# Seven products instead of eight for the second matrices of two MLPs

## The chip, the cores and the metric

One core of a Trainium2 chip runs the whole program, in float32. The metric is the time of one execution on the device, in microseconds (us); smaller is better.

## What is computed

A first block (attention and a layer of 16 experts) is followed by a second block of two layers. Each layer of the second block mixes 256 tokens of width 1024 and then applies an MLP with a hidden width of 4096. The change touches only the two MLPs on the 256 tokens:

```python
def _mlp(h, w1, w2):
    return jnp.square(jax.nn.relu(h @ w1)) @ w2
...
        x = _layer_norm(alpha * x + g2 * _mlp(x * (1 + sc2) + sh2, mlp_w1[i], mlp_w2[i]), ln2_g[i], ln2_b[i])
```

h is 256 x 1024, w1 is 1024 x 4096, w2 is 4096 x 1024.

## The kernel before

TensorE (PE) multiplies, VectorE (DVE), ScalarE (ACT) and GpSimd (POOL) do the rest, SyncE (SP) issues the weight transfers. Every engine has its own program, executed in order; the order is written out by hand, and engines wait for each other on counting semaphores. All weights go through `ring`, 8 slots of 3072 columns; `feed` issues the transfer of piece n as soon as piece n - 8 is released (`released`), and `arrived` is the wait for a piece. PSUM, the target of the matmuls, has 8 banks of 512 columns. `link` makes DVE wait for its own operation, for where the next one reads its result.

The function `mlp` (L2267) is called twice: for the first layer as mlp_x (about 1884 to 2100 us), for the second as mlp_n (about 2287 us to the end). The hidden width is cut into GROUPS = 16 groups of 256 columns, each with a piece of w1 (`ids[1, g]`, 8 x 256 columns of a slot) and a piece of w2 (`ids[2, g]`, 2 x 1024 columns). LATE = 3 groups at the end are treated apart, so that the first half of the tokens is finished while PE still works on the second.

The first matrix is multiplied by Strassen's scheme in Winograd's form: tokens (2 halves), inner width (2 halves) and the group's columns (2 halves) make 2 x 2 blocks, and seven block products stand for eight. Their operands are the blocks of the transposed tokens `H` and four sums of them `T[1]` to `T[4]` (made once, L2376 to L2379), and the blocks `W` of the weights and four sums (made by DVE for each group in `add_weights`, L2386 to L2390). Two sums lie in the slot behind the piece, one over block 21, the fourth in `fourth`. A block product is four matmuls of 128 columns, since the inner half width is 512. `first(g)` on PE issues the seven products, 28 matmuls, into two banks: 0 and 1 for even groups, 2 and 3 for odd ones. `combine(g)` on DVE adds the products into the four blocks of the hidden layer (L2402 to L2406), then relu and square go into `h1` in one operation (L2412).

The second matrix is multiplied directly: `second(g, t, half)` (L2327) multiplies 128 tokens with 512 output columns in two matmuls of 512 columns, one for each 128 of the group's inner width. The four combinations of t and half add up over all groups in banks 4 to 7. PE's order is first(0), then for each g first(g+1) and the four second(g). In the last three groups only t = 0 is done in this loop, and t = 1 follows, one half after the other.

DVE's order is the weight sums of g+1, then combine(g). After group 8 (GROUPS // 2) `ln_gain` multiplies the residual x by the gain of the layer norm before it and adds the shift, two operations of 1024 columns for each of the two token tiles. At the end DVE multiplies each bank by the gate `gB`, adds ALPHA times x (`gated`, L1542 and L1543), takes statistics and normalizes.

Of the kernel before, what the change touches and what calls it, by code (L numbers as in the profile page):

```python
# [120 lines left out]
def build(nc, A):  # L121
    ctx = ExitStack()
    with nc.Block(no_gpsimd_drain=True) as block, ctx:
# [39 lines left out]
        combined = Count(sem("mlp_combined"))  # L163
        square_done = Count(sem("square_done"))
# [2102 lines left out]
        def mlp(name, layer, s, ids, banks_free, input_normed, prefetch=None, beside=None, tail=None, finish=None):  # L2267
# [4 lines left out]
            fourth = sb(f"{name}_fourth", [2, 4, P], st)  # L2272
# [7 lines left out]
            tsb, wsb, fb, cb, qb = (turned_sums.take(1), weight_sums.take(2 * GROUPS), first_done.take(GROUPS),  # L2280
                                    combined.take(GROUPS), square_done.take(GROUPS))
# [5 lines left out]
            def weights(g):  # L2287

                w = slot(ids[1, g], KC * 2 * P).rearrange("p (k f) -> p k f", k=KC)
                rest = ring[:, ids[1, g] % SLOTS, KC * 2 * P:SLOT].rearrange("p (i k f) -> p i k f", i=2, k=4)  # L2290
                W = {"11": w[:, upper, here], "12": w[:, lower, here], "21": w[:, upper, there], "22": w[:, lower, there]}
                sums = {1: rest[:, 0, :, :], 2: rest[:, 1, :, :], 3: W["21"], 4: fourth[:, g % 2, :, :]}
                return W, sums

            @block.tensor
            def _(pe):
# [5 lines left out]
                def first(g):  # L2302
                    arrived(pe, ids[1, g])
                    if g >= 2:
                        pe.wait_ge(combined.sem, cb + g - 1)
                    W, sums = weights(g)
                    bank = 2 * (g % 2)
                    for n, (b, at, lhs, rhs) in enumerate(((0, 0, W["11"], H["11"]), (0, 1, W["12"], H["21"]),
                                                           (1, 2, W["22"], T[4]), (0, 3, sums[3], T[3]),
                                                           (1, 0, sums[1], T[1]), (0, 2, sums[2], T[2]),  # L2310
                                                           (1, 1, sums[4], H["22"]))):
                        if n == 2 and g == 0:
                            pe.wait_ge(turned_sums.sem, tsb + 1)
                        if n == 3:
                            pe.wait_ge(weight_sums.sem, wsb + 2 * g + 1)
                        if n == 6:
                            pe.wait_ge(weight_sums.sem, wsb + 2 * g + 2)
                        for k in range(4):
                            last = nc.tensor.matmul(ps[:, bank + b, at * P:at * P + P], lhs[:, k, :], rhs[:, k, :],  # L2319
                                                    start=(k == 0), stop=(k == 3), skip_group_check=True)  # L2320
                    last.then_inc(first_done.sem, 1)
                    released[ids[1, g]] = (first_done.sem, fb + g + 1)

                def second(g, t, half):
                    w2 = slot(ids[2, g], 2 * D).rearrange("p (k f) -> p k f", k=2)
                    for fc in range(2):
                        last = nc.tensor.matmul(ps[:, 4 + 2 * t + half, :], h1[:, g % 4, fc, t * P:(t + 1) * P],  # L2327
                                                w2[:, fc, 512 * half:512 * half + 512], start=(g == 0 and fc == 0),
# [3 lines left out]
                early = GROUPS - LATE  # L2332
                first(0)
                for g in range(GROUPS):
                    if g + 1 < GROUPS:
                        first(g + 1)
                    arrived(pe, ids[2, g])
                    pe.wait_ge(square_done.sem, qb + g + 1)
                    if g == 0:
                        banks_free(pe)  # L2340
                    for t in range(NT if g < early else 1):
                        for half in range(2):
                            last = second(g, t, half)
                    if g < early:
                        last.then_inc(mlp_used.sem, 1)
                        released[ids[2, g]] = (mlp_used.sem, used + g + 1)
                last.then_inc(mlp_used.sem, 1)
                for half in range(2):
                    for g in range(early, GROUPS):
                        last = second(g, 1, half)  # L2350
                    last.then_inc(mlp_used.sem, 1)
                for g in range(early, GROUPS):
                    released[ids[2, g]] = (mlp_used.sem, used + early + 3)
# [19 lines left out]
            def _(dve):  # L2373
                run_t.ev(dve, "dve")
                run_t.finished(dve)
                nc.vector.tensor_tensor(T[1], H["12"], H["11"], ALU.subtract)  # L2376
                link(dve, nc.vector.tensor_tensor(T[3], H["22"], H["12"], ALU.subtract))
                link(dve, nc.vector.tensor_tensor(T[2], H["22"], T[1], ALU.subtract))
                nc.vector.tensor_tensor(T[4], H["21"], T[2], ALU.subtract).then_inc(turned_sums.sem, 1)  # L2379

                def add_weights(g):
                    arrived(dve, ids[1, g])
                    if g >= 2:
                        dve.wait_ge(first_done.sem, fb + g - 1)
                    W, sums = weights(g)
                    nc.vector.tensor_tensor(sums[1], W["21"], W["22"], ALU.add)  # L2386
                    link(dve, nc.vector.tensor_tensor(sums[3], W["11"], W["21"], ALU.subtract))
                    nc.vector.tensor_tensor(sums[2], sums[1], W["11"], ALU.subtract).then_inc(weight_sums.sem, 1)
                    dve.wait_ge(weight_sums.sem, wsb + 2 * g + 1)
# [336 lines left out]
```

## Time and profile before

| what | us |
|---|---|
| median of 3 runs | 2513.24 (2512.06 to 2516.07) |
| the profiled execution | 2514.77 |
| its span | 2513.0 |
| PE busy in the span | 2188.3 |
| DVE busy in the span | 682.7 |
| PE, L2327, mlp_x and mlp_n | 112.3 and 112.4 |

The span is the time from the first to the last instruction in the profiled execution, and the profile's times count from its start. A float32 matmul stands in the records as two matmuls and two weight loads (PEld), so 128 matmuls of L2327 in one MLP are 256 records. The granted clock is given as a share of full speed: 1.00 is 2.4 GHz, 0.50 is 1.2 GHz, and between them lies a stretch that had both.

### The profile page before, as it was taken

To read this page: it belongs to the slowest core of one execution; us is meant where nothing else is said; L and a number is where in the kernel's file an instruction comes from. 1 tells how busy PE (TensorE), PEld (TensorE's weight loads), DVE (VectorE), ACT (ScalarE), POOL (GpSimd) and SP (SyncE) were. 2 spreads that over 40 slices of the span, in tenths; PEclk is the share of its full clock that TensorE was granted. 3 is DMA by queue.
4 is the path that set the end of the run, shared out by engine and by line. 5 is a ranking of instruction groups with operands and counts; after the bars stand their busy time and mean duration, and the time that the engine had idled before them with its cause. 6 is when DMAs were issued, how large, how long until landed. Compare 5 with 4: busy or idle time off the path is not lost.

```text
span 2513.0 us, 29663 instructions
## 1 busy us (share of the span) xinstructions
PE 2188.3 (87%) x12828; PEld 1189.4 (47%) x12828; DVE 682.7 (27%) x1319; ACT 211.4 (8%) x495; POOL 41.4 (2%) x109
## 2 busy tenths in 40 slices
PE   8988889878768978978978977978999999989998
PEld 6544353333323424433433424435557776646775
DVE  1332212221311021021011032022335434075344
ACT  1221110000100000000000000011110000060000
POOL 0000000000000000000000000000000003000000
PEclk9999999989899989999999999989899999999999
DMA  8879999999999999999999999993218554324450
GB/s 314 335 280 390 420 407 424 424 424 422 424 420 419 415 420 412 416 419 413 414 420 417 413 424 422 398 415 116 97 48 257 172 188 184 138 90 143 158 177 34
DMA packets 154819, 799.52 MB, mean 318 GB/s; under 512 B 15587, under 2 KB 71626, under 8 KB 101634
## 3 DMA queue, kind: packets, MB, share of 16 engines
q1 hardware_dynamic: 144504, 783.43, 77.5%
q10 hardware_dynamic: 10186, 14.16, 1.7%
q8 instruction: 108, 1.77, 0.3%
q14 instruction: 21, 0.17, 0.0%
HBM read 795.40 MB, written 7.19 MB: 319 GB/s over the span
## 4 chain that ended last, share of the span: by engine, by line
PE 70%; DMA 17%; DVE 7%; issue 3%; ACT 2%; SPq 1%; ACTq 0%; DVEq 0%
PE ps L288 12%; PE ps L1868 8%; PE ps L2327 8%; PE ps L2319 8%; DMA ring<-in_mlp_w 7%; PE ps L321 6%; PE ps L1836 5%; PE ps L2038 4%; PE ps L1841 3%; DMA ring<-in_w_up 3%; PE ps L418 2%; PE ps L1889 2%; PE ps L1877 2%; DVE expert_work L1911 2%; PE ps L2030 2%
## 5 line engine op out<-in xcount | busy, mean ns | idle before, releaser
L1836 PE MATMUL ps<-ring,xe 128*32 128x512 f32 x2048 | 297.2, 643 | 84.4 <-DMA ring<-in_w_up 30.2
L1868 PE MATMUL ps<-ring,expert_work 128*32 128x512 f32 x1408 | 236.4, 688 | 11.5 <-ACT expert_work L1898 11.0
L1841 PE MATMUL ps<-ring,xe 128*32 128x256 f32 x2048 | 207.3, 464 | 2.8 <-issue 2.8
L1841 PEld LDWEIGHTS ps<-ring,xe 128*32 128x32 f32 x2048 | 74.8, 111 | 174.0 <-issue 173.1
L1836 PEld LDWEIGHTS ps<-ring,xe 128*32 128x32 f32 x2048 | 61.4, 114 | 191.4 <-issue 94.6
L1868 PEld LDWEIGHTS ps<-ring,expert_work 128*32 128x32 f32 x1408 | 59.0, 121 | 155.0 <-issue 132.0
L2038 PE MATMUL ps<-ring,c_qT 128*128 128x512 f32 x256 | 114.1, 598 | 11.2 <-DMA ring<-in_mlp_w 11.2
L2030 PE MATMUL ps<-hT,ring 128*128 128x256 f32 x512 | 114.8, 382 | 6.6 <-DMA ring<-in_mlp_w 6.6
L2327 PE MATMUL ps<-ring,mlp_n_h 128*128 128x512 f32 x256 | 112.4, 592 | 0.0
L2327 PE MATMUL ps<-ring,mlp_x_h 128*128 128x512 f32 x256 | 112.3, 592 | 0.0
L2030 PEld LDWEIGHTS ps<-hT,ring 128*128 128x128 f32 x512 | 96.0, 190 | 28.5 <-DMA ring<-in_mlp_w 11.0
L1848 PE MATMUL ps<-cst,expert_work 128*128 128x128 f32 x64 | 18.1, 436 | 96.6 <-DVE expert_work L1915 96.6
L2152 DVE TENSOR_TENSOR c_qT<-c_qT 128x512 f32<-128x512 f32 x16 | 11.1, 693 | 323.6 <-ACT c_qT L2102 323.6
L321 PE MATMUL ps<-hT,ring 128*128 128x256 f32 x384 | 84.1, 380 | 3.2 <-DMA ring<-in_na_w_qkv 2.2
L2038 PEld LDWEIGHTS ps<-ring,c_qT 128*128 128x128 f32 x256 | 47.3, 190 | 74.6 <-issue 74.6
L1911 DVE RECIPROCAL expert_work<-expert_work 128x512 f32<-128x512 f32 (+1 forms) x32 | 81.7, 2553 | 1.1
L321 PEld LDWEIGHTS ps<-hT,ring 128*128 128x128 f32 x384 | 72.5, 190 | 16.6 <-issue 6.9
L1909 DVE TENSOR_SCALAR expert_work<-expert_work 128x512 f32<-128x512 f32 (+1 forms) x32 | 11.3, 354 | 242.6 <-ACT expert_work L1895 242.6
L1889 PE MATMUL ps<-expert_work,gs 128*128 128x512 f32 x128 | 60.6, 618 | 18.9 <-DVE expert_work L1924 18.9
L2327 PEld LDWEIGHTS ps<-ring,mlp_x_h 128*128 128x128 f32 x256 | 47.5, 190 | 54.1 <-issue 54.1
L2327 PEld LDWEIGHTS ps<-ring,mlp_n_h 128*128 128x128 f32 x256 | 47.5, 190 | 54.1 <-issue 54.1
L1877 PEld LDWEIGHTS ps<-chosen,h 128*128 128x128 f32 x512 | 59.1, 194 | 13.0 <-issue 12.9
(424 smaller groups left out, 2489.1 us busy)
## 6 DMA issues: line engine op xcount, KB each, us to landing
ring<-in_w_gate SPq DMA_DIRECT2D x128, 1408.0 KB, 17.9
ring<-in_w_up SPq DMA_DIRECT2D x128, 1408.0 KB, 17.8
ring<-in_w_down SPq DMA_DIRECT2D x112, 1536.0 KB, 23.7
ring<-in_mlp_w SPq DMA_DIRECT2D x96, 1024.0 KB, 7.4
ring<-in_ada_w SPq DMA_DIRECT2D x32, 1536.0 KB, 10.3
ring<-in_na_w_qkv SPq DMA_DIRECT2D x20, 1024.0 KB, 13.7
ring<-in_w_in SPq DMA_DIRECT2D x8, 1536.0 KB, 21.0
ring<-in_w_down SPq DMA_DIRECT2D x16, 512.0 KB, 23.7
```

The source lines that it names most:

```text
L288: last = nc.tensor.matmul(bank[0:rows, lo:hi], lhsT, rhs, start=start, stop=stop)
L321: last = nc.tensor.matmul(self.part(i), lhsT, rhs, start=(k == 0 and i % self.per == 0), stop=(k == depth - 1), skip_group_check=True)
L1836: nc.tensor.matmul(ps[32 * j:32 * j + 32, up, :], xe[:, k, :], w[:, :, 4 * j:4 * j + 4], start=(k == 0), stop=(k == KC - 1))
L1841: last = nc.tensor.matmul(ps[32 * j:32 * j + 32, 2, 256 * up:256 * up + 256], xe[:, k, :], two, start=(k == 0 and not up), stop=(k == KC - ...
L1868: last = nc.tensor.matmul(ps[32 * j:32 * j + 32, 1 - half, :], hgT[:, at:at + 32], w[:, (c - c0) * D + 512 * half:(c - c0) * D + 512 * hal ...
L1877: nc.tensor.matmul(ps[:, 3, lo:hi], lhsT, rhs, start=start, stop=stop)
L1889: last = nc.tensor.matmul(ps[:, 2 * t + half, :], gs[:, t * P:(t + 1) * P], ye[:, 512 * half:512 * half + 512], start=True, stop=True)
L1911: nc.vector.reciprocal(part, part).then_inc(e_own, 1)
L2030: last = nc.tensor.matmul(ps[:, 3, S * fc:S * fc + S], w1[:, k, fc * P:(fc + 1) * P], buf["hT"][:, k, :], start=(k == 0), stop=(k == KC - 1))
L2038: last = nc.tensor.matmul(ps[:, CB[2 * t + half], :], m_h1[:, g, S * fc + t * P:S * fc + (t + 1) * P], w2[:, fc, 512 * half:512 * half + 512],
L2319: last = nc.tensor.matmul(ps[:, bank + b, at * P:at * P + P], lhs[:, k, :], rhs[:, k, :], start=(k == 0), stop=(k == 3), skip_group_check= ...
L2327: last = nc.tensor.matmul(ps[:, 4 + 2 * t + half, :], h1[:, g % 4, fc, t * P:(t + 1) * P], w2[:, fc, 512 * half:512 * half + 512], start=( ...
```

## The change

Groups 0 to 12 (SEVEN = 13) multiply the second matrix by seven products too. The 2 x 2 blocks are two halves of tokens, of the group's 256 inner columns and of the 1024 output columns; a block product is one matmul of 512 columns. Its operands: blocks of `h1` and four sums of them (`h1_sums`), blocks of w2 and four sums (two in the slot behind the piece, one over block 12, the fourth in `fourth2`), all made by DVE in `value_operands(g)`. Each of the seven products adds up over the 13 groups in a bank of its own, banks 1 to 7. Only after that are the products added into the four output blocks: `fold_first` and `fold_rest` on DVE, which already apply the gate and add to ALPHA times x. Groups 13 to 15 use `second` as before, into banks 4 to 7 anew, and the end of the function adds them by a multiplication with the gate and an addition.

The first matrix has bank 0 alone now (bank 7 for the second round of group 0), and so goes in two rounds: `first(g, 0)` with four products, `first(g, 1)` with three. Between them DVE reads the bank (`combine_first`), after them too (`combine_rest`). `fourth` has one buffer instead of two. PE's order per group is first(g+1, 0), products(g, 0), first(g+1, 1), products(g, 1), with four and three products.

```diff
+                def first(g, turn):
                     W, sums = weights(g)
+                    if turn == 0:
+                        arrived(pe, ids[1, g])
+                        if g:
+                            pe.wait_ge(combined.sem, cb + (2 * g if g > 1 else 1))
+                        bank, products = 0, ((W["11"], H["11"], 0), (W["12"], H["21"], 0), (sums[3], T[3], 1), (sums[2], T[2], 2))
+                    else:
+                        if g:
+                            pe.wait_ge(combined.sem, cb + 2 * g + 1)
+                        bank, products = (0 if g else 7), ((sums[1], T[1], 2), (sums[4], H["22"], 3), (W["22"], T[4], 3))
+                    for at, (lhs, rhs, ready) in enumerate(products):
+                        if ready:
+                            pe.wait_ge(weight_sums.sem, wsb + 3 * g + ready)
...
+                def products(g, turn):
+                    A11, A21, A12, A22 = (h1[:, g % 4, fc, t * P:t * P + P] for fc in range(2) for t in range(NT))
+                    W, sums = value_weights(g)
+                    S1, S2, S3, S4 = (h1_sums[:, g % 2, i, :] for i in range(4))
+                    if turn == 0:
+                        arrived(pe, ids[2, g])
+                        pe.wait_ge(square_done.sem, qb + g + 1)
+                        todo = ((4, A11, W["11"]), (5, A12, W["21"]), (7, S3, sums[3]), (6, S2, sums[2]))
+                    else:
+                        todo = ((1, S1, sums[1]), (2, S4, W["22"]), (3, A22, sums[4]))
+                    for n, (bank, lhsT, rhs) in enumerate(todo):
+                        if turn == 0 and n == 2:
+                            pe.wait_ge(value_sums.sem, vsb + g + 1)
+                        last = nc.tensor.matmul(ps[:, bank, :], lhsT, rhs, start=(g == 0), stop=(g == SEVEN - 1),
+                                                skip_group_check=True)
...
                 def second(g, t, half):
+                    if (t, half) == (0, 0):
+                        arrived(pe, ids[2, g])
+                        pe.wait_ge(square_done.sem, qb + g + 1)
+                    if g == SEVEN:
+                        pe.wait_ge(folded.sem, ob + 2 * t + half + 1)
...
+                banks_free(pe)
+                first(0, 0)
+                first(0, 1)
                 for g in range(GROUPS):
+                    for turn in range(2):
+                        if g + 1 < GROUPS:
+                            first(g + 1, turn)
+                        if g < SEVEN:
+                            products(g, turn)
+                        else:
+                            last = second(g, 0, turn)
...
+                def combine_first(g):
+                    b = ps[:, 0, :]
+                    dve.wait_ge(first_done.sem, fb + 2 * g + 1)
+                    link(dve, nc.vector.tensor_copy(parts[:, 7, :], b[:, 0:P]))
+                    plus(parts[:, 6, :], parts[:, 7, :], b[:, 3 * P:4 * P])
+                    link(dve, plus(parts[:, 0, :], parts[:, 7, :], b[:, P:2 * P]))
+                    plus(parts[:, 5, :], parts[:, 6, :], b[:, 2 * P:3 * P]).then_inc(combined.sem, 1)
+
+                def combine_rest(g):
+                    b = ps[:, 0 if g else 7, :]
+                    dve.wait_ge(first_done.sem, fb + 2 * g + 2)
+                    dve.wait_ge(combined.sem, cb + 2 * g + 1)
+                    link(dve, plus(parts[:, 3:5, :], parts[:, 5:7, :], both(b[:, 0:P])))
+                    plus(parts[:, 1:3, :], parts[:, 4:6, :], two(b[:, P:3 * P])).then_inc(combined.sem, 1)
+                    dve.wait_ge(combined.sem, cb + 2 * g + 2)
                     if g >= 4:
                         dve.wait_ge(mlp_used.sem, used + g - 3)
                     c = parts[:, 0:4, :].rearrange("p i s -> p (i s)")
                     nc.vector.scalar_tensor_tensor(h1[:, g % 4, :, :].rearrange("p a b -> p (a b)"), c, 0.0, c, ALU.max, ALU.mult)\
                       .then_inc(square_done.sem, 1)
+                def value_operands(g):
+                    if g >= 2:
+                        dve.wait_ge(mlp_used.sem, used + g - 1)
+                    dve.wait_ge(square_done.sem, qb + g + 1)
+                    A11, A21, A12, A22 = (h1[:, g % 4, fc, t * P:t * P + P] for fc in range(2) for t in range(NT))
+                    S1, S2, S3, S4 = (h1_sums[:, g % 2, i, :] for i in range(4))
+                    plus(S1, A21, A22)
+                    link(dve, minus(S3, A11, A21))
+                    link(dve, minus(S2, S1, A11))
+                    minus(S4, A12, S2)
+                    arrived(dve, ids[2, g])
+                    W, sums = value_weights(g)
+                    minus(sums[1], W["12"], W["11"])
+                    link(dve, minus(sums[3], W["22"], W["12"]))
+                    link(dve, minus(sums[2], W["22"], sums[1]))
+                    minus(sums[4], W["21"], sums[2]).then_inc(value_sums.sem, 1)
+
+                a_part, b_part = fourth2[:, 0, :], fourth2[:, 1, :]
+
+                def update(y, t, half):
+                    part, gate = x[:, t, 512 * half:512 * half + 512], gB[:, 512 * half:512 * half + 512]
+                    link(dve, nc.vector.tensor_tensor(y, y, gate, ALU.mult))
+                    return nc.vector.scalar_tensor_tensor(part, part, ALPHA, y, ALU.mult, ALU.add)
+
+                def fold_first():
+                    dve.wait_ge(mlp_used.sem, used + SEVEN)
+                    dve.wait_ge(v.sem, v.at("gain"))
+                    dve.wait_ge(gate_loaded.sem, gate_loaded.n)
+                    nc.vector.tensor_copy(a_part, ps[:, 4, :]).then_inc(folded.sem, 1)
+                    dve.wait_ge(folded.sem, ob + 1)
+                    plus(b_part, a_part, ps[:, 5, :]).then_inc(folded.sem, 1)
+                    dve.wait_ge(folded.sem, ob + 2)
+                    link(dve, update(b_part, 0, 0))
+                    plus(a_part, a_part, ps[:, 6, :]).then_inc(folded.sem, 1)
+                    dve.wait_ge(folded.sem, ob + 3)
+                    plus(b_part, a_part, ps[:, 7, :]).then_inc(folded.sem, 1)
+
+                def fold_rest():
+                    dve.wait_ge(folded.sem, ob + 4)
+                    link(dve, plus(a_part, a_part, ps[:, 1, :]))
+                    link(dve, plus(a_part, a_part, ps[:, 2, :]))
+                    link(dve, update(a_part, 0, 1))
+                    link(dve, plus(a_part, b_part, ps[:, 1, :]))
+                    link(dve, update(a_part, 1, 1))
+                    link(dve, plus(b_part, b_part, ps[:, 3, :]))
+                    update(b_part, 1, 0).then_inc(folded.sem, 1)
...
+                minus(T[1], H["12"], H["11"])
+                minus(T[3], H["22"], H["12"]).then_inc(turned_sums.sem, 1)
+                first_sums(0)
+                dve.wait_ge(turned_sums.sem, tsb + 1)
+                minus(T[2], H["22"], T[1]).then_inc(turned_sums.sem, 1)
+                second_sum(0)
+                dve.wait_ge(turned_sums.sem, tsb + 2)
+                minus(T[4], H["21"], T[2]).then_inc(turned_sums.sem, 1)
+                last_sum(0)
                 if tail:
                     fold_ln(dve, fold, 1, layer, layer + 1, 0)
                 for g in range(GROUPS):
+                    combine_first(g)
                     if g + 1 < GROUPS:
+                        first_sums(g + 1)
+                        second_sum(g + 1)
+                    if g == SEVEN + 1:
+                        fold_rest()
+                    combine_rest(g)
+                    if g < SEVEN:
+                        value_operands(g)
+                    if g + 1 < GROUPS:
+                        last_sum(g + 1)
+                    if g == SEVEN:
+                        fold_first()
                     if g == GROUPS // 2:
                         dve.wait_ge(ln_loaded.sem, ln1_loaded)
                         for t in range(NT):
                             last = ln_gain(dve, x, t)
```

`first_sums(g)` makes the sums 1 and 3 of w1's blocks, `second_sum(g)` sum 2 and `last_sum(g)` sum 4, each an operation of 512 columns as in `add_weights`.

## Rows read from the trace of the kernel before

**Rows 1.** Engines' busy time, of the page.
```profile
PE 2188.3 (87%) x12828; PEld 1189.4 (47%) x12828; DVE 682.7 (27%) x1319; ACT 211.4 (8%) x495; POOL 41.4 (2%) x109
```

**Rows 2.** The chain of waits, 1880 to 2110 us (start, length, what).
```profile
1890.99 12.02 PE ps L2319 x96
1903.01 6.87 PE ps L2327 x16
1909.88 6.25 PE ps L2319 x56
...
2083.25 17.18 PE ps L2327 x40
```

**Rows 3.** Timeline of one group of mlp_x (start us, us, engine, line, operation).
```profile
1942.20 7.03 PE L2327 MATMUL ps<-ring,mlp_x_h 128*128 128x512 f32 x16
1942.40 0.29 DVE L2402 COPY mlp_x_parts<-ps 128x128 f32<-128x128 f32 x1 [7.76 <-PE ps L2319]
...
1942.73 0.42 DVE L2403 TENSOR_TENSOR mlp_x_parts<-ps,mlp_x_parts 128x256 f32<-128x256 f32 x1
...
1943.19 0.29 DVE L2404 TENSOR_TENSOR mlp_x_parts<-mlp_x_parts,ps 128x128 f32<-128x128 f32 x1
...
1943.51 0.42 DVE L2405 TENSOR_TENSOR mlp_x_parts<-mlp_x_parts,ps 128x256 f32<-128x256 f32 x1
...
1944.42 0.69 DVE L2412 SCALAR_TENSOR_TENSOR mlp_x_h<-mlp_x_parts 128x512 f32<-128x512 f32 x1
...
1945.03 0.68 DVE L2386 TENSOR_TENSOR ring<-ring 128x512 f32<-128x512 f32 x1
...
1945.63 0.68 DVE L2387 TENSOR_TENSOR ring<-ring 128x512 f32<-128x512 f32 x1
...
1946.35 0.69 DVE L2388 TENSOR_TENSOR ring<-ring 128x512 f32<-128x512 f32 x1
```

**Rows 4.** Timeline of VectorE in mlp_x around group 8.
```profile
1997.51 1.22 DVE L853 TENSOR_TENSOR x<-x,lnb 128x1024 f32<-128x1024 f32 x1
...
2002.30 0.68 DVE L2386 TENSOR_TENSOR ring<-ring 128x512 f32<-128x512 f32 x1
...
2008.00 0.29 DVE L2402 COPY mlp_x_parts<-ps 128x128 f32<-128x128 f32 x1 [2.97 <-PE ps L2319]
```

**Rows 5.** Timeline of the starts of mlp_x and mlp_n.
```profile
1888.18 0.69 DVE L2376 TENSOR_TENSOR mlp_x_tokens<-mlp_x_hT 128x512 f32<-128x512 f32 x1 [0.56 <-ACT mlp_x_hT L357]
...
1890.24 0.69 DVE L2379 TENSOR_TENSOR mlp_x_tokens<-mlp_x_hT,mlp_x_tokens 128x512 f32<-128x512 f32 x1
...
1890.99 4.87 PE L2319 MATMUL ps<-mlp_x_tokens,ring 128*128 128x128 f32 x32 [0.17 <-DVE mlp_x_tokens L2379]
...
1902.84 3.60 PE L2327 MATMUL ps<-ring,mlp_x_h 128*128 128x512 f32 x8
...
2290.74 0.69 DVE L2376 TENSOR_TENSOR mlp_n_tokens<-mlp_n_hT 128x512 f32<-128x512 f32 x1 [0.46 <-DVE mlp_n_hT L369]
...
2305.51 2.74 PE L2327 MATMUL ps<-ring,mlp_n_h 128*128 128x512 f32 x6
```

**Rows 6.** Groups of instructions of 1880 to 2110 us.
```profile
L1542 DVE TENSOR_TENSOR ps<-ps,mlp_x_gate 128x512 f32<-128x512 f32 x4 | 2.8, 694 | 6.5 <-PE ps L2327 6.5
```

**Rows 7.** Stretches: length, busy PE, PEld, DVE, ACT, POOL, granted clock, DMA.
```profile
279.93:283.30 3.37, 2.68 (x12) 1.14 (x15) 2.75 (x4) 2.14 (x6) 0.00 (x0) 0.50 1.00 423
283.30:286.70 3.40, 3.40 (x20) 0.80 (x13) 0.00 (x0) 0.81 (x4) 0.00 (x0) 0.71 1.01 425
...
304.00:308.00 4.00, 1.50 (x11) 0.37 (x13) 2.35 (x2) 0.00 (x0) 0.00 (x0) 1.00 1.01 424
...
1888.20:1890.80 2.60, 2.60 (x16) 2.31 (x16) 2.53 (x4) 0.00 (x0) 0.00 (x0) 0.76 1.09 315
1890.98:1892.90 1.92, 1.91 (x8) 1.78 (x8) 1.85 (x4) 0.00 (x0) 0.00 (x0) 0.50 1.05 323
```

**Rows 8.** Timeline of TensorE at the first expert's hidden layer.
```profile
279.93 1.13 PE L1848 MATMUL ps<-cst,expert_work 128*128 128x128 f32 x4 [6.02 <-DVE expert_work L1915]
```

More of the change, by code:

```diff
@@ L2300, in _ @@
                 run_t.finished(pe)
[L2302 to L2305, printed above, removed]
+                def first(g, turn):
                     W, sums = weights(g)
[L2307 to L2317, printed above, removed]
+                    if turn == 0:
[10 more added lines that the diff above has]
+                            pe.wait_ge(weight_sums.sem, wsb + 3 * g + ready)
+                            if g == 0:
+                                pe.wait_ge(turned_sums.sem, tsb + ready)
@@ L2327, in second @@
                         last = nc.tensor.matmul(ps[:, 4 + 2 * t + half, :], h1[:, g % 4, fc, t * P:(t + 1) * P],
-                                                w2[:, fc, 512 * half:512 * half + 512], start=(g == 0 and fc == 0),
+                                                w2[:, fc, 512 * half:512 * half + 512], start=(g == SEVEN and fc == 0),
                                                 stop=(g == GROUPS - 1 and fc == 1), skip_group_check=True)
                     return last
-                early = GROUPS - LATE
-                first(0)
+                banks_free(pe)
+                first(0, 0)
+                first(0, 1)
                 for g in range(GROUPS):
[L2335 to L2346, printed above, removed]
+                    for turn in range(2):
[5 more added lines that the diff above has]
+                            last = second(g, 0, turn)
                 last.then_inc(mlp_used.sem, 1)
                 for half in range(2):
-                    for g in range(early, GROUPS):
+                    for g in range(SEVEN, GROUPS):
                         last = second(g, 1, half)
                     last.then_inc(mlp_used.sem, 1)
-                for g in range(early, GROUPS):
-                    released[ids[2, g]] = (mlp_used.sem, used + early + 3)
+                for g in range(SEVEN, GROUPS):
+                    released[ids[2, g]] = (mlp_used.sem, used + SEVEN + 3)
+                pe.wait_ge(folded.sem, ob + 5)
                 if beside:
@@ new lines, in first_sums, with second_sum, last_sum @@
+                    plus(sums[1], W["21"], W["22"])
+                    minus(sums[3], W["11"], W["21"]).then_inc(weight_sums.sem, 1)
+                def second_sum(g):
+                    W, sums = weights(g)
+                    dve.wait_ge(weight_sums.sem, wsb + 3 * g + 1)
+                    minus(sums[2], sums[1], W["11"]).then_inc(weight_sums.sem, 1)
+                def last_sum(g):
+                    W, sums = weights(g)
+                    dve.wait_ge(weight_sums.sem, wsb + 3 * g + 2)
+                    minus(sums[4], W["12"], sums[2]).then_inc(weight_sums.sem, 1)
```

76 lines of the change are left out of this document (35 added, 41 removed).

## The prediction

> **What bounds the kernel now.** I read the page first: TensorE (PE) is busy 87% of the span [rows 1]. An average over stages says little, so I cut out the two MLPs, from 1880 to 2110 us (mlp_x) and from 2290 us to the end (mlp_n), and read the chain of waits. In mlp_x it is PE from end to end: 12.02 us for the 48 small matmuls that begin before the first `second`, then 6.87 us and 6.25 us in turn with nothing between them, 17.18 us at the end [rows 2]. The reader should see two numbers: 16 records, that is 8 matmuls of 512 columns, take 6.87 us, so one takes 0.859; 56 records, 28 matmuls of 128 columns, take 6.25 us, so one takes 0.223. A group costs 13.12 us. The timeline of one group shows VectorE (DVE) idle 7.76 us per group, waiting for PE [rows 3]. So any matmul less is time won, as long as DVE keeps up.
>
> DVE's pace I read as start-to-start distances [rows 3]. 512 elements: 0.60 us if the next instruction does not wait for it (1945.03 to 1945.63), 0.72 if it does (1945.63 to 1946.35). 256 elements with a wait 0.46 (1942.73 to 1943.19), 128 elements 0.33 (a copy) and 0.32. A 128-element operation that nobody waits for does not occur; by the 512 pair's difference of 0.09 to 0.12 I take 0.21 (bounds 0.18, and 0.32 if nothing overlaps). PE's last matmul is seen by DVE 0.20 us after the next matmul could have started (1942.20 to 1942.40) [rows 3]. For the other direction the start of mlp_x shows 0.06 us: T4 ends at 1890.93, its matmul begins at 1890.99 [rows 5]. There PE had just been busy; behind a longer wait I take 0.15 (bounds 0.06 and 0.3).
>
> **The change, step by step.** I write F0 for the first round of a group's first matrix (4 products of 4 matmuls, 16 x 0.223 = 3.57 us), F1 for the second (12, 2.68), P0 and P1 for the rounds of `products` (4 and 3 matmuls: 3.44 and 2.58). A group is now 12.27 instead of 13.12.
>
> *Gain.* Thirteen groups lose one 512-column matmul each: 12 x 0.859 = 10.31 us for groups 1 to 12; group 0 is counted with the start. The additional waits of PE (about 11 per group instead of 5) I cost at nothing while they are satisfied: the 6.25 us hold four such waits and are still 28 x 0.223.
>
> *Steady state.* Count from the end of F1(g), PE at 0. PE does P1(g-1) until 2.58, F0(g+1) until 6.15, P0(g) until 9.59. DVE sees F1 at 0.20, `combine_rest` has read the bank at 1.08 (needed at 2.58), the square ends at 1.80 (needed at 6.15), the four token sums take 0.21+0.32+0.32+0.21 from 1.84, the four weight sums begin at 2.90 and the last ends at 5.63 (needed at P0's third matmul, 7.87). `last_sum` begins at 5.54, `combine_first(g+1)` at F0's sight, 6.35, and ends 1.15 later, at 7.50 (needed at 9.59). Two sums and `second_sum` fill until about 9.4; F1(g+1) ends at 12.27. DVE has 8.9 us of issue in a 12.27 us period and every operand comes 1.5 us or more early. PE stays unbroken here. The price if DVE were late by d in each group: 24 x d. The ring's transfers are hidden: two pieces per group are wanted now by DVE instead of PE, but the slot releases come as often as before and there was no DMA in the chain [rows 2].
>
> *Start.* DVE works 8 sums in a new order from 1888.18 [rows 5]: `sums[3]` is ready at 1890.7, `sums[2]` with T2 at 1891.9, T4 1892.5, `sums[4]` 1893.1. PE spends the first two products until 1890.8 at a clock of 0.76 and the third at 0.50 [rows 7]; F0(0) ends at 1893.6, F1(0) at 1896.2, about as before. What is late then is DVE: `combine_first(0)` from 1893.8 (1.15 us), three weight sums of group 1 (1.32 + 0.60), `combine_rest(0)` and the square from 1896.8 until 1898.4, the eight value operands until 1902.2. P0(0) wants them at 1896.2 + 3.57 + 1.72 = 1901.5 and gets them at 1902.4: a stall of 0.9 us (bounds 0 and 2, an error of two DVE operations either way). P0(0), F1(1) and P1(0) end at 1909.35, against 1902.84 + 6.87 = 1909.71 before: 0.36 won instead of 0.86. In mlp_n the same from 2290.74 gives 2312.3 against 2305.51 + 6.87 = 2312.38: 0.08 [rows 5].
>
> *The layer-norm gain after group 8.* Its four DVE operations take 4.79 us from 1997.51 to 2002.30, and DVE still idles 2.97 us after them [rows 4]. That cover is gone. `last_sum(9)` begins at 5.54, the gain at 6.14, `combine_first(9)` at 10.93, ends 12.08, F1(9) can start at 12.23 instead of 9.59: 2.64 us lost, per MLP. After it the steady state is restored.
>
> *Folding.* DVE has to put the seven banks together, 6 operations in `fold_first` and 10 in `fold_rest`, 512 columns each. One such with a PSUM operand takes 0.69 [rows 6], as those in SBUF do, so I space them by 0.72 (bounds 0.60 and 0.78). Count from the end of P1(12). PE: F0(14) to 3.57, `second(13,0,0)` to 5.29, then F1(14), which waits for `combine_first(14)`. DVE: the six of `fold_first` start at 0.20, 0.93, 1.65, 2.37, 3.09 and 3.81; the bank that `second(13,0,0)` overwrites is copied by 0.9, in time. Then `combine_first(14)` 4.41 to 5.56. F1(14) starts 5.71: 0.42 lost. It ends 8.39, `second(13,0,1)` 10.11. Next on PE is F0(15), which waits for `combine_rest(14)`, and that stands on DVE behind `fold_rest`: sums of group 15 from 5.48, `fold_rest` from 7.40, ten times 0.72 less 0.12 = 7.08, `combine_rest(14)` from 14.48, bank read at 15.36, F0(15) at 15.51. **5.40 us lost**, with all of PE's queue behind it. The square of group 15 is late by another 0.23. Sum 6.05 per MLP; the spacing's bounds make it 3.6 to 6.9. The end itself, multiply, add and statistics per half, has as many operations as before.
>
> *The clock.* After 6.02 us of idleness in dense work [rows 8] PE's stretches ran 3.37 us at 0.50 and 3.40 us at 0.71 [rows 7]: 1.69 + 0.99 = 2.7 us of work lost. The 4.00 us from 304, of which PE worked only 1.50, read 1.00 [rows 7]. At mlp_x's start 2.60 us at 0.76 and 1.92 at 0.50 lost 1.6. For 5.40 us I take 1.8, between 1.6 and 2.7 and nearer the first as the idle time is shorter; bounds 0 and 2.7. For 2.64 us I take 0, bounds 0 and 2.7.
>
> The Trainium skill ("TensorE: Matmul & The Clock Gate", "Loop structure matters more than you think") says that long waits of PE between matmuls send it back to half rate; this speaks against the change where `fold_rest` stands. The trace agrees in the row after 6.02 us. Read strictly for every stall here it would give the slow rival below. The skill also says ("VectorE: DVE Perf Modes", "Terms") that a DVE operation cannot issue until the one before has left the pipe; the trace shows 0.60 us starts for 0.68 us operations and disagrees. By the rule the gain's stall would be some 0.6 us longer.
>
> *Sum.* Two MLPs: 20.62 + 0.36 + 0.08 - 2 x 2.64 - 2 x 6.05 - 2 x 1.8 = 0.1 us won. The profiled execution (2514.77, its span 2513.0) would read 2514.7; the median of the runs lies 1.5 below it, so I say 2513.2.
>
> **Rivals.** Two tenths of a per cent, 5 us, is about what a measurement of this kernel can tell from no change.
> - *No loss of clock at the fold.* The same stalls, 3.6 us less: 2509.6. For it: the 2.50 us case. Against: the 6.02 us case. Chance 0.15, still within 5 us.
> - *The stalls do not appear*, because PE is queued further or the fold is beside work I missed: 22.3 us less, 2491; with only the 5.40 us hidden and its clock loss gone, 2513.2 - 14.4 = 2499. For it: DVE idles 7.76 us a group. Against: DVE and PE work in order, and both waits are written in their queues. Chance 0.1.
> - *Slower: the short stalls drop the clock too.* The place is F1(9) after 2.64 us of idleness; price up to 2.7 per MLP, and the fold at 2.7 instead of 1.8: 2513.2 + 5.4 + 1.8 = 2520.4. It decides from the point where 2.64 us of idleness is enough. For it: at mlp_x's start, with work and pauses in turn before it, the clock fell to 0.50; against: 4.00 us with only 1.50 of work stayed at 1.00 [rows 7]. Chance 0.17, two thirds of it over 2518.3.
> - *DVE's or PE's small costs:* 0.2 us more per group by waits or operands late, 24 groups, 4.8 us: 2518. For it: nothing seen; against: the 1.5 us of slack. Chance 0.08.
>
> **The numbers.** Forecast 0.50. The range 2505 to 2519.5 takes in the clock's bounds and errors of 1 us in each stall, and leaves out most of the hidden-stall case and the end of the slow one. Faster by over 0.2%: 0.10 from the hidden stalls, 0.08 from forecast and no-loss case with smaller stalls: 0.18. Slower: 0.11 + 0.04 + 0.03 = 0.18. Within: 0.64.
>
> **What would show it.** In the chain of mlp_x after: pieces of PE of 12.27 us per group without idle from group 2 to 8; one wait of PE of about 2.6 us for the parts of `combine_first` after the gain; one of about 5.4 us for the parts of `combine_rest` behind ten DVE operations; a granted clock of 0.5 behind the latter. PE's busy time falls by about 22 us less what half clock adds, while the span hardly moves. I am wrong if PE waits in the steady state, if the 5.4 us are not there, or if the clock drops behind the short stalls.

## The result and the profile after

Nine runs of each kernel gave a median of 2521.4 us (2518.21 to 2525.36) after the change and 2514.75 us (2512.06 to 2520.19) before. The ratio is 1.0024, 95% interval 1.0014 to 1.0034: 6.0 us slower, 3.5 to 8.6. The forecast was 2513.2 in a range of 2505 to 2519.5. A later comparison of the same two kernels, 12 and 35 runs, gave 1.0010 (0.9999 to 1.0020), 2.5 us, with an interval that reaches from nothing to 5.0; the medians there, 2521.58 and 2516.83 us, lie 4.8 apart.

The page of the profiled execution (2521.4 us): the span is 6.6 us longer, while PE is busy 3.6 us less than before [rows 1]. In the two MLPs it is busy 12.5 us less, outside them 8.9 us more, where its matmuls are the same; there this time was 1761 to 1776 us in the five profiles with the old order of PE and 1765 to 1785 in the nine with the new one.

```profile
span 2519.6 us, 29905 instructions
...
PE 2184.7 (87%) x12776; PEld 1194.8 (47%) x12776; DVE 797.8 (32%) x1591; ACT 211.5 (8%) x495; POOL 41.3 (2%) x109
```

The chain of waits in mlp_x after (start, length, what), answering to [rows 2]. L2332 is now the first matrix, L2351 `products`, L2365 `second`.

```profile
1910.83 3.57 PE ps L2332 x32
1914.40 3.44 PE ps L2351 x8
1917.84 2.68 PE ps L2332 x24
1920.51 2.58 PE ps L2351 x6
...
1991.40 2.69 PE ps L2332 x24
...
2006.12 4.57 PE ps L2332 x24
...
2077.68 5.77 PE ps L2332 x32
2083.46 1.72 PE ps L2365 x4
2085.17 2.68 PE ps L2332 x24
```

The first four lines are one group: 3.57, 3.44, 2.68, 2.58, together 12.27 us, without a gap, against 13.12 before. The fifth is F1(8), a second round as it should be. The sixth is F1(9), the same 24 records, and takes 4.57 us instead of 2.68. The seventh is F0(15): 32 records in 5.77 us instead of 3.57. The eighth and ninth, behind it, have their normal lengths again.

A piece in dense work is counted here from the end of the matmul before it, which lies 0.16 us behind the start of its own first matmul; a piece behind a pause is counted from that start. From start to start F1(9) therefore takes 4.41 us and F0(15) 5.61, that is 1.73 and 2.04 us more than in dense work. These are the figures used below, since the pauses are taken from start to start too (2.61 us where the record has 2.45 of idle time).

The timelines (start, us, engine, line, operation, idle before) show what came before the sixth and the seventh. PE at group 9:

```profile
2001.79 1.88 PE L2351 MATMUL ps<-ring,mlp_x_h_sums 128*128 128x512 f32 x4
2006.12 1.57 PE L2332 MATMUL ps<-mlp_x_tokens,ring 128*128 128x128 f32 x8 [2.45 <-DVE mlp_x_parts L2415]
```

VectorE over the same stretch, to be read beside [rows 4]:

```profile
2000.15 1.22 DVE L855 TENSOR_TENSOR x<-x,lnb 128x1024 f32<-128x1024 f32 x1
2001.40 1.23 DVE L856 TENSOR_TENSOR x<-x,lnb 128x1024 f32<-128x1024 f32 x1
2002.55 1.22 DVE L855 TENSOR_TENSOR x<-x,lnb 128x1024 f32<-128x1024 f32 x1
2003.80 1.22 DVE L856 TENSOR_TENSOR x<-x,lnb 128x1024 f32<-128x1024 f32 x1
2004.94 0.28 DVE L2442 COPY mlp_x_parts<-ps 128x128 f32<-128x128 f32 x1
```

PE's last matmul of P0(8) leaves room for a next one at 2003.5. The four gain operations run from 2000.15 on, and the copy that begins `combine_first(9)` starts at 2004.94 without any idle time before it, where before VectorE idled 2.97 us. PE idles 2.45 us by the record, 2.6 from 2003.5 to 2006.12.

PE at the fold, then VectorE:

```profile
2067.76 1.16 PE L2332 MATMUL ps<-mlp_x_tokens,ring 128*128 128x128 f32 x8 [0.15 <-DVE mlp_x_parts L2415]
...
2070.54 1.88 PE L2365 MATMUL ps<-ring,mlp_x_h 128*128 128x512 f32 x4
2077.68 2.69 PE L2332 MATMUL ps<-mlp_x_hT,ring 128*128 128x128 f32 x11 [5.26 <-DVE mlp_x_parts L2415]
```

```profile
2062.35 0.69 DVE L2488 COPY mlp_x_fourth<-ps 128x512 f32<-128x512 f32 x1 [0.37 <-PE ps L2351]
...
2069.55 1.40 DVE L2415 TENSOR_TENSOR mlp_x_fourth<-mlp_x_fourth,ps 128x512 f32<-128x512 f32 x2
...
2076.06 0.69 DVE L2482 SCALAR_TENSOR_TENSOR x<-x,mlp_x_fourth 128x512 f32<-128x512 f32 x1
2076.67 0.87 DVE L2415 TENSOR_TENSOR mlp_x_parts<-mlp_x_parts,ps 128x256 f32<-128x256 f32 x2
```

Of the sixteen fold operations the first, the first of `fold_rest` and the last are shown. The last starts at 2076.06, `combine_rest(14)` right behind it at 2076.67, and PE's F0(15) at 2077.68 after 5.26 us of idleness.

The stretches behind the two stalls, with the long stall itself in the second line (length, busy PE, PEld, DVE, ACT, POOL, granted clock, DMA share, GB/s), answering to [rows 7]:

```profile
2006.12:2010.70 4.58, 4.58 (x25) 4.58 (x26) 1.84 (x3) 0.00 (x0) 0.00 (x0) 0.63 0.68 223
2072.30:2077.68 5.38, 0.12 (x1) 0.03 (x1) 5.10 (x10) 0.00 (x0) 0.00 (x0) 0.75 0.61 254
2077.68:2081.10 3.42, 3.42 (x16) 3.42 (x17) 1.19 (x2) 0.00 (x0) 0.00 (x0) 0.50 0.00 0
2081.10:2083.46 2.36, 2.36 (x19) 2.36 (x19) 0.00 (x0) 0.00 (x0) 0.00 (x0) 0.85 0.00 0
2083.46:2103.60 20.14, 20.07 (x68) 9.90 (x71) 9.99 (x20) 0.20 (x1) 0.00 (x0) 1.00 0.00 1
```

Behind the short stall 4.58 us at 0.63, behind the long one 3.42 us at 0.50 and 2.36 us at 0.85: 1.7 us and 2.1 us of work lost, the same sizes as by the pieces. In both places the clock is at 1.2 GHz instead of 2.4 GHz for a while, although PE has nothing but dense work behind the stall. Over the long stall itself the clock reads 0.75: it had fallen before the stall was over, and the part of the slow time in which PE had nothing to do cost nothing.

Where the 6.6 us of span lie, by the first and last matmul of each MLP:

| | before | after | difference |
|---|---|---|---|
| up to mlp_x's first matmul | 1888.20 | 1889.45 | 1.25 |
| mlp_x | 212.22 | 214.16 | 1.94 |
| between the MLPs | 189.97 | 191.06 | 1.09 |
| mlp_n | 212.70 | 215.06 | 2.36 |

The rest of the span, behind mlp_n, differs by less than 0.1. Mlp_x by terms, each from start to start: 12 x 0.859 = 10.31 and 0.30 at the start won; lost 2.61 (gain), 1.73 (its clock), 0.41 (before and in F1(14)), 5.43 (fold), 2.04 (its clock), 0.32 (the late square of group 15). That is 12.54 - 10.61 = 1.93, as measured. In mlp_n the start loses 0.06 instead.

### The profile page after: what moved, and what is told of

The parts are those of the page before. It is cut to its first block, busy times and chain, and to the rows that moved or that the text cites. A ratio compares the mean times of both kernels' runs of the same rounds, so it can differ in the third digit from the quotient of the medians.

```text
span 2519.6 us, 29905 instructions
## 1 busy us (share of the span) xinstructions
PE 2184.7 (87%) x12776; PEld 1194.8 (47%) x12776; DVE 797.8 (32%) x1591; ACT 211.5 (8%) x495; POOL 41.3 (2%) x109
## 4 chain that ended last, share of the span: by engine, by line
PE 68%; DMA 16%; DVE 10%; issue 3%; ACT 2%; SPq 1%; ACTq 0%; DVEq 0%
PE ps L290 12%; PE ps L1870 9%; PE ps L2332 7%; DMA ring<-in_mlp_w 7%; PE ps L323 6%; PE ps L1838 6%; PE ps L2351 6%; PE ps L2040 4%; PE ps L1843 3%; DMA ring<-in_w_up 3%; PE ps L420 2%; PE ps L1891 2%; PE ps L1879 2%; DVE expert_work L1913 2%; PE ps L2032 2%
## 5 line engine op out<-in xcount | busy, mean ns | idle before, releaser
L2412 DVE TENSOR_TENSOR ring<-ring 128x512 f32<-128x512 f32 x142 | 95.4, 687 | 1.9
L2332 PE MATMUL ps<-mlp_x_tokens,ring 128*128 128x128 f32 x512 | 67.2, 281 | 2.6 <-DVE mlp_x_parts L2415 2.6
L2332 PE MATMUL ps<-mlp_n_tokens,ring 128*128 128x128 f32 x512 | 67.2, 281 | 2.6 <-DVE mlp_n_parts L2415 2.6
L2332 PEld LDWEIGHTS ps<-mlp_n_tokens,ring 128*128 128x128 f32 x512 | 64.3, 198 | 10.5 <-issue 5.3
L2332 PEld LDWEIGHTS ps<-mlp_x_tokens,ring 128*128 128x128 f32 x512 | 64.1, 198 | 10.6 <-issue 5.3
```

The costliest lines, as they stand in the source:

```text
L2332: last = nc.tensor.matmul(ps[:, bank, at * P:at * P + P], lhs[:, k, :], rhs[:, k, :], start=(k == 0), stop=(k == 3), skip_group_check=True)
L2412: return nc.vector.tensor_tensor(out, a, b, ALU.subtract)
```

## The experiments

The theory (A): the matmuls saved are worth their full 22 us, and VectorE's order gives them back in two stalls per MLP, each with a loss of clock behind it where the clock falls. The main rivals: only the idle time counts and the clock falls anyway (B); VectorE is simply too full, so that a stall would move and not go (C); the matmul saved is worth less.

**The changed kernel again**, without an edit.

> The changed kernel once more, for a second profile. Theory A: the stall of TensorE before F1(9), about 2.6 us, and that before F0(15), about 5.4 us, come again in both MLPs, since they follow from VectorE's order alone; the granted clock behind them may differ, as the clock's changes are not tied to the kernel: 0 to 2 us behind the short stall, 1 to 2.7 behind the long one. Rival B: the difference of 6.6 us between the first two profiles lies outside the MLPs in good part (1.25 us before mlp_x, 1.1 between the MLPs) and comes from the changed code: then these two offsets come again with the same size.

2519.39 us. MLPs of 212.08 and 215.28 us, 1889.59 up to the first and 190.7 between. The stalls came again (7.9 us of PE waiting for `parts` in each MLP, 5.3 the longest), but not the clock's fall behind every one: in mlp_x F1(9) took 2.94 us, in mlp_n 4.57. From its chain of waits:

```profile
2005.86 2.94 PE ps L2332 x24
```

So the same idle time costs 0.1 us or 1.7 us behind it, from start to start, and that makes 1.6 us of difference between two executions. The two offsets outside the MLPs came again too, 1.4 and 0.7 us, as the rival B of this run has it; the runs at the end of this section take that up.

**The gain moved.**

```diff
-                    if g == GROUPS // 2:
-                        dve.wait_ge(ln_loaded.sem, ln1_loaded)
-                        for t in range(NT):
-                            last = ln_gain(dve, x, t)
-                        last.then_inc(v.sem, v("gain"))
+                    if g == GROUPS // 2:
+                        dve.wait_ge(ln_loaded.sem, ln1_loaded)
+                        ln_gain(dve, x, 0)
+                    if g == GROUPS // 2 + 1:
+                        ln_gain(dve, x, 1).then_inc(v.sem, v("gain"))
                     combine_rest(g)
```

> Only the four gain operations are moved: two stand before combine_rest of group 8, two before that of group 9, where VectorE waits for TensorE about 3 us. Theory A (the stall of 2.6 us and the clock it costs, 1.9 us, in each MLP): 9.0 us less than the changed kernel, about 2512.4; TensorE unbroken from group 2 to 12 and the granted clock 1.00 there. Rival B (the clock falls in this stretch anyway): 5.2 us less. Rival C (VectorE is too full, the stall moves to another group): 0 to 3 us less.

2511.82 us median of 10; ratio to the kernel before 0.9984 (0.9970 to 0.9999). 9.6 us less than the changed kernel's 2521.4, though the two intervals together leave some 4 us either way, so that the time alone does not tell 9.0 from rival B's 5.2. The profile does: MLPs of 209.06 and 211.04 us, together 9.1 us less than in the first profile of the changed kernel and 7.3 less than in the second, where the clock had fallen behind one short stall and not two. The list of waits has only the fold's left (waited for: total, times, longest):

```profile
PE ps L2332 <- DVE mlp_x_parts L2415: 5.4, 2, 5.3
```

No second round longer than 2.7 us is in its chain from group 2 to 12, and the granted clock is 1.00 there. The stall went and did not move, which speaks against C.

**The fold spread.** The sixteen operations in the same order, cut into five parts (the comments are added here).

```diff
+                    if g == SEVEN + 1:
+                        fold_more()      # a += bank 6, b = a + bank 7
+                    if g == SEVEN + 2:
+                        fold_rest(1)     # bank 1 and the update of (1, 1)
                     combine_rest(g)
...
                     if g == SEVEN:
                         fold_first()     # banks 4 and 5, the update of (0, 0)
+                    if g == SEVEN + 1:
+                        fold_rest(0)     # banks 1 and 2, the update of (0, 1)
+                    if g == SEVEN + 2:
+                        fold_rest(2)     # bank 3, the update of (1, 0)
```

> Only the folding is spread: of the sixteen operations four stay after last_sum(14), two go before combine_rest(14), four after last_sum(15), three before and three after combine_rest(15). Theory A (5.4 us of stall, 2.2 of clock, 0.3 and 0.1 of small waits in each MLP): 16 us less than the changed kernel, about 2505.4. Rival B (only the idle time comes back, the clock not): 11.6 us less. Rival C: what is moved behind combine_rest(15) delays the end, where the gate is applied: 1 to 3 us of the gain are given back in each MLP.

2506.33 us median of 7; ratio 0.9953 (0.9936 to 0.9969). 15 us less than the changed kernel. MLPs of 204.3 and 204.2 us. What is left in its waits is the gain's stall alone:

```profile
PE ps L2332 <- DVE mlp_x_parts L2415: 2.5, 1, 2.5
```

The clock behind it stayed up in both MLPs (2.94 us for F1(9)). The MLPs are 20.7 us shorter together than in the first profile of the changed kernel, where 16 were expected; 3.3 of that is this luck with the clock behind the short stall, and 1.3 lie at the start of mlp_n. Nothing was given back at the end.

**Both.**

> Both moves together. Theory A: 25 us less than the changed kernel, about 2496.4, and 18 to 19 less than the kernel before, since only the start's 0.9 us stays lost of the 22.3 us that 26 matmuls of 0.859 us are worth. Rival B: 16.8 less than the changed kernel, about 2504.6. Rival C (the matmul saved is worth less than 0.859 us when nothing else is in the way): the steady period is over 12.3 us.

2495.7 us median of 6, ratio 0.9912 (0.9892 to 0.9932): 22 us faster than the kernel before by the ratio (17 to 27), 20 by the medians, 26 less than the changed one; this version beats both. MLPs of 202.0 and 203.0 us, 19.9 less together than before the change, where 18 to 19 were expected. PE from group 2 to the end of mlp_x, then VectorE at group 8:

```profile
1910.00:2091.00 181.00, 180.88 (x1002) 128.70 (x1001) 136.26 (x281) 0.20 (x1) 0.00 (x0) 1.00 0.52 184
```

```profile
1991.20 1.22 DVE L855 TENSOR_TENSOR x<-x,lnb 128x1024 f32<-128x1024 f32 x1
1992.45 1.23 DVE L856 TENSOR_TENSOR x<-x,lnb 128x1024 f32<-128x1024 f32 x1
1994.33 0.88 DVE L2415 TENSOR_TENSOR mlp_x_parts<-mlp_x_parts,ps 128x256 f32<-128x256 f32 x2 [0.66 <-PE ps L2332]
```

180.88 of 181.00 us busy at a clock of 1.00. In the timeline the first tile's gain sits before `combine_rest(8)`, and VectorE still idles 0.66 us after it. VectorE is busy 136 of the 181 us, with the gain's and the folding's operations in them, so it was not too full for them.

**The fold moved by one place**, from before `combine_rest(14)` to after `last_sum(15)`.

```diff
-                    if g == SEVEN + 1:
-                        fold_rest()
                     combine_rest(g)
...
+                    if g == SEVEN + 1:
+                        fold_rest()
```

> The changed kernel with one line moved: fold_rest stands after last_sum(15) instead of before combine_rest(14). The same ten operations. Theory A (the stall is the place in VectorE's order): TensorE no longer waits before F0(15); it waits before F1(15) for combine_first(15), which now stands behind fold_rest, about 3.7 us instead of 5.4. 1.5 us less per MLP and about the same clock loss behind it: 3 us less than the changed kernel in all. Rival B (ten more operations cost their 7 us wherever they stand): a stall of 5 us or more.

2512.04 us, MLPs of 209.98 and 209.94. Where the stall is went as A said, from F0(15) to F1(15), and is 3.44 us long:

```profile
2071.93 1.95 PE L2332 MATMUL ps<-mlp_x_hT,ring 128*128 128x128 f32 x16
...
2080.82 1.32 PE L2332 MATMUL ps<-mlp_x_tokens,ring 128*128 128x128 f32 x8 [3.44 <-DVE mlp_x_parts L2415]
```

In the chain of waits F1(15) is one piece of 24 records, 1.7 us longer than in dense work by its clock:

```profile
2080.82 4.57 PE ps L2332 x24
```

The MLPs are 7.4 us shorter together than in the second profile of the changed kernel, not 3. The two stalls are 1.8 us shorter each (3.6), the clock behind them costs 1.7 instead of 2.0 and 2.2 (0.7). The other 3.1 us are luck: behind the gain the clock stayed up in both MLPs, where the other profile lost 1.6 in one, and the start of mlp_n was 1.4 us faster. The direction was right; of the size two fifths are luck.

**Three gain operations instead of four**, on the kernel with both moves.

```diff
+                    if g == GROUPS // 2:
+                        dve.wait_ge(ln_loaded.sem, ln1_loaded)
+                        ln_gain(dve, x, 0)
+                        link(dve, nc.vector.tensor_tensor(x[:, 1, :], x[:, 1, :], lnb[:, 0, :], ALU.mult))
...
```

> The kernel with both moves, but three of the four gain operations stand together after last_sum(9), the fourth before combine_rest(9): a shorter stall before F1(9). Theory A: 2.6 - 1.2 = 1.4 us of stall in each MLP, and the clock stays at 1.00 behind it (F1(9) takes 2.7 to 2.9 us). Rival B (any pause costs clock in proportion): F1(9) takes about 3.7 us. Against the kernel with both moves 2.8 us more by A, 4.8 by B.

2501.21 us. The stall is 1.3 us by the record, 1.5 from start to start, and F1(9) takes 2.94 us in both MLPs; the MLPs are 3.2 us longer together than with both moves (408.25 against 405.02). PE at the stall:

```profile
2005.61 1.16 PE L2332 MATMUL ps<-mlp_x_tokens,ring 128*128 128x128 f32 x8 [1.30 <-DVE mlp_x_parts L2415]
2006.61 1.06 PE L2332 MATMUL ps<-mlp_x_hT,mlp_x_fourth 128*128 128x128 f32 x8
```

The second product after it already has its full pace: the loss does not grow in proportion, as B has it. That a pause this short never lowers the clock is not shown; these are two cases, and of the 2.5 us pauses six of ten kept it too.

**An eighth matmul**, on the kernel with both moves.

```diff
-                        todo = ((1, S1, sums[1]), (2, S4, W["22"]), (3, A22, sums[4]))
+                        todo = ((1, S1, sums[1]), (2, S4, W["22"]), (3, A22, sums[4]), (3, A22, sums[4]))
...
```

The flag `start` is adjusted with it, so that the additional matmul adds to its bank.

> The kernel with both moves, and one matmul of 512 columns more in the second round of each of the 13 groups of both MLPs (the product of bank 3 is added twice, so the output blocks with it are not the reference's). Theory A: each costs 0.859 us, 26 of them 22.3 us: 2495.7 + 22.3 = 2518.0, a period of 13.12 us. Rival B (part of it would be hidden behind waits): the period is under 13.0.

2520.8 us median of 10, ratio 1.0018 (1.0007 to 1.0030). Its chain has periods of 13.12 us, without a gap:

```profile
1947.48 3.57 PE ps L2332 x32
1951.05 3.44 PE ps L2351 x8
1954.48 2.68 PE ps L2332 x24
1957.16 3.44 PE ps L2351 x8
```

Beside both moves that is 3.44 instead of 2.58 in the fourth piece of each group, 0.86 us each, and 25 us in the medians where 22.3 was expected; the MLPs, 212.75 us each, are 20.5 us longer together. The missing 1.8 lie ahead of P1(0), where nothing was added: with another clock at the start this profile gets there 0.45 and 1.39 us sooner in the two MLPs. The value of the saved matmul is as predicted.

**What lies outside the MLPs.** With the eighth matmul the MLPs are as long as before the change, and yet the kernel came out 4.5 us slower (1.8 to 7.5). So I looked for a cost of the change elsewhere: the kernel before against itself, then with the additional names only, then with a busier VectorE.

> The kernel before once more, for a second profile. Theory A: the MLPs take 212.2 and 212.7 us again, and what lies before mlp_x and between the MLPs differs from the first profile by about 1 us, as it does among the five profiles of changed kernels (189.3 to 191.4 us between the MLPs). Rival B: 190.0 between them and 1888.2 at the start come again, so that the changed kernels' larger values belong to the change.

2513.4 us; 1886.97 up to mlp_x, 189.56 between.

> The kernel before against itself, to see what a comparison of this length says of no change. By both theories 0 us. If it comes out 2 us or more off, the part of the difference outside the MLPs (theory A: chance) is within what the measurement can do.

Ratio 0.9992 (0.9980 to 1.0004).

```diff
+        value_sums = Count(sem("mlp_value_sums"))
+        folded = Count(sem("mlp_folded"))
...
+            pad = sb(f"{name}_pad", [3, 512], st)
```

> The kernel before with the two additional semaphores and with the 1536 additional columns of SBUF per MLP of the change, unused. Theory A (what the changed kernels lose outside the MLPs is chance): 0 us. Rival B (numbering of the semaphores or placement in SBUF costs time outside the MLPs): 2 to 4 us more.

Ratio 0.9990 (0.9978 to 1.0001).

```diff
...
+                    if 0 < g < GROUPS - LATE and g != GROUPS // 2:
+                        for i in range(6):
+                            link(dve, nc.vector.tensor_tensor(pad[:, 1 + i % 2, :], pad[:, 0, :], pad[:, 0, :], ALU.add))
```

> As the one before, and six operations of 512 columns more on VectorE in 11 groups of each MLP, where VectorE idles 7.8 us (they add a tile of zeros to itself and nothing reads the result). TensorE's order is the old one. Theory A: 0 us, the MLPs at 212.2 and 212.7 us. Rival C (a busier VectorE or a longer program slows the rest): 2 to 4 us more, seen in the profile either as a longer period than 13.12 us or outside the MLPs.

Ratio 0.9998 (0.9984 to 1.0011), MLPs of 212.22 and 212.95 us.

> The changed kernel timed beside these three. By the profiles' terms for the MLPs alone (10.3 + 0.3 won; 2.6, 5.4 and 0.4 of stalls, about 0.9 and 2.2 of clock lost, per MLP) 2 us more than the kernel before; by the first comparison 6.

Ratio 1.0010 (0.9999 to 1.0020), MLPs of 212.05 and 214.98 us. The names cost nothing: 2 to 4 us are outside their interval. For the busier VectorE no cost is seen, in the MLPs or in the ratio, but its interval reaches to 2.8 us, so that only the larger part of the rival's 2 to 4 is excluded. Mlp_x began at 1887.0 to 1896.4 us in the five profiles that have the old order of PE, and at 1886.3 to 1895.9 in the nine of changed kernels; between the MLPs lay 189.2 to 191.0 and 189.3 to 193.0 us. This scatter is larger than the 2.3 us in the table above. Between the MLPs it goes with the clock, as the 35 us behind mlp_x show, first in the kernel before, then in the changed one (columns as above):

```profile
2100.42:2135.42 35.00, 29.79 (x183) 22.89 (x183) 15.98 (x23) 2.13 (x5) 20.26 (x24) 1.00 0.75 285
2103.61:2138.61 35.00, 29.70 (x174) 22.52 (x175) 15.58 (x22) 2.13 (x5) 20.24 (x24) 0.95 0.75 285
```

Where this stretch reads 1.00, 189.2 to 190.0 us lie between the MLPs; where it reads 0.95, 190.7 to 191.4; with the eighth matmul it read 0.90, and 193.0 us. It read 1.00 in four of the five profiles with the old order of PE and in two of the nine with the new one. These are too few to say whether the change makes the fall more frequent, and no run separates that from chance: whether a part of the time lost outside the MLPs belongs to the change stays open.

## Why the prediction was wrong

- *Gain of the matmuls and steady state:* right. 12.27 us per group, no idle time, and 0.86 us per group come back when the eighth is put in again.
- *Start:* right in size. 0.6 us of stall by the record at P0(0), 0.76 from start to start, where 0.9 was worked out; 0.30 us won in mlp_x where 0.36 was expected, 0.06 lost in mlp_n where 0.08 was to be won.
- *Layer-norm gain:* right. 2.6 us predicted, 2.6 measured.
- *Folding:* right. 5.40 us predicted before F0(15), 5.43 measured; 0.42 before F1(14), 0.31; 0.23 for the square, 0.23. The place was right, and the two runs that moved the folding show it. Not foreseen was a small cost of any pause at a full clock: the piece behind it takes 0.1 us longer from start to start.
- *The clock:* this is the step that failed, a term of the sum that was mis-sized. "For 5.40 us I take 1.8" and "For 2.64 us I take 0": 3.6 us for both MLPs. In the profiled execution it was 2.0 and 2.1 behind the long stalls and 1.7 and 1.7 behind the short ones: 7.6 us. That is 4.0 of the 4.4 us by which the MLPs missed the forecast in this execution. Over all profiles with these stalls the long one cost 1.7 to 2.5 us in 8 of 8 cases, 2.1 in the mean, and the short one 1.7 in 4 of 10 and 0.1 in 6 of 10, 0.75 in the mean. With these means the MLPs lose 2.3 us together instead of winning 0.1. The three profiles of the changed kernel have 427.0 to 429.2 us in the two MLPs, the five with the old order 424.9 to 425.3: 2.8 us more in the mean.
- The row from which the long stall's term was taken was read too high: of its first 3.37 us PE worked 2.68 [rows 7], so 1.34 + 0.99 = 2.3 us of work were lost and not 2.7. With 1.8 taken and 2.1 measured this did little harm.
- The rival "slower: the short stalls drop the clock too", priced at 2520.4 with a chance of 0.17, is what the profiled execution did in its MLPs. Its 2.7 us behind each stall are more than the 2.0 and 1.7 measured, and it comes near the median of 2521.4 only because of time outside the MLPs. I had put its chance too low because one pause of similar length, at 304 us, kept the clock [rows 7]; one case decided a term that differs from one execution to the next.
- *Range:* it was said to take in the clock's bounds, but these, 2.7 us behind each stall, give the 2520.4 of the slow rival and so lie outside its upper end. The remaining 2.3 us of the profiles' difference lie outside the MLPs. The comparison at first gave 6.0 us and later 2.5, where the MLPs account for 2 to 3; what made up the rest the first time stays open. The range had 6.3 us of room above, but was centred on a median of three runs that nine and then 35 runs put at 2514.75 and 2516.83. The changed kernel is slightly slower in the first comparison; the second, with an interval from 0.9999, does not tell it from no change, and no change within 0.2% was the likeliest case of the forecast.

The Trainium skill's warning that long waits between matmuls send PE back to half rate ("TensorE: Matmul & The Clock Gate", "Loop structure matters more than you think") agrees with the long stalls here: the clock fell in all 8 cases. Behind the short ones it fell in 4 of 10.

## What to carry to other kernels

When an idle helper engine is given work, look through its queue for everything rare that stood there for free: two rare pieces of work, 4.8 us and 7.1 us of VectorE in each MLP, took back all that 26 matmuls brought. Cutting them into pieces that fit the gaps of each group, with the same operations, made of a change that won nothing one that wins 0.9%. Price a stall of TensorE in dense work as the idle time plus the clock behind it, and where the traces of before show both outcomes, carry that as chance and not as zero.

## What was not expected of the hardware

How the price of a pause in dense float32 matmuls grows, from start to start: behind 1.3 us of idleness 0.1 us were lost (2 cases), behind 2.5 us 0.1 or 1.7 us (6 and 4 cases), behind 3.4 us 1.7 us (2 cases), behind 5.3 us 1.7 to 2.5 us (8 cases). The 0.1 us is there at a clock of 1.00 too: 24 records take 2.78 us behind such a pause instead of 2.68. The same pause in the same place of the same program can cost 0.1 us in one execution and 1.7 in the next, and the clock can fall while PE still stands (0.75 over the long stall), so that only a part of the slow time is paid for.
